# A value mix moved behind the first inverse set-up, and the last chunk's steps in another order

## What is computed

```python
prev = jnp.pad(zb, ((0, 0), (1, 0), (0, 0)))[:, :T]
zb = zb + (prev - zb) * mu
r, k, v, xw, xa, xg = jnp.split(zb, cuts, axis=-1)
...
y = wkv7_scan(heads(r), heads(decay), heads(k), heads(v), -kk, kk * heads(a))
...
def step(S, inp):
    r_t, w_t, k_t, v_t, a_t, b_t = inp
    sa = jnp.einsum('bhvk,bhk->bhv', S, a_t)
    S = S * w_t[:, :, None, :] + sa[..., None] * b_t[:, :, None, :] + v_t[..., None] * k_t[:, :, None, :]
    y = jnp.einsum('bhvk,bhk->bhv', S, r_t)
    return S, y
```

## Time and profile before

| | |
|---|---|
| median of three runs | 2555.91 us (2554.29 to 2558.12) |
| the profiled execution | 2555.16 us |
| its span | 2553.4 us |
| PE busy | 2489.6 us, 98% of the span |
| DVE busy | 1428.8 us, 56% |
| ACT busy | 1093.3 us, 43% |
| POOL busy | 147.6 us, 6% |
| last slab's matmuls end | about 327 us |
| recurrence alone on the engines | about 327 to 446 us |

### The profile page before, as it was taken

How to read it: one execution, slowest core, us unless ns; L and a number is a source line. 1 busy time by engine, 2 the same in 40 slices (tenths; PEclk the granted TensorE clock), 3 DMA queues, 4 the chain that set the end, 5 groups by cost and what they waited for, 6 DMA issues and landing times.

```text
span 2553.4 us, 31712 instructions
## 1 busy us (share of the span) xinstructions
PE 2489.6 (98%) x13463; PEld 2056.5 (81%) x13463; DVE 1428.8 (56%) x1555; ACT 1093.3 (43%) x1216; POOL 147.6 (6%) x171
## 2 busy tenths in 40 slices
PE   8999999999999999999998999999999999999998
PEld 6888778778888888888777977777888888888876
DVE  5556775665445545455556667656545444545564
ACT  5445432454434334334445445554434434334442
POOL 4001224000000000000000000000000000000100
PEclk9999999999999999999999999999999999999999
DMA  8556511546565555555553654356555565555543
GB/s 262 191 180 207 172 31 69 198 170 230 182 197 181 197 188 185 190 196 182 181 181 116 207 164 151 116 165 225 190 189 192 182 197 184 194 189 190 183 169 127
DMA packets 224850, 453.22 MB, mean 177 GB/s; under 512 B 7865, under 2 KB 16375, under 8 KB 223435
## 3 DMA queue, kind: packets, MB, share of 16 engines
q1 hardware_dynamic: 219165, 430.63, 50.7%
q0 software_dynamic: 3648, 17.54, 2.2%
q10 hardware_dynamic: 1902, 3.07, 0.4%
HBM read 445.52 MB, written 2.10 MB: 175 GB/s over the span
## 4 chain that ended last, share of the span: by engine, by line
PE 92%; DVE 4%; ACT 2%; DMA 1%; issue 1%; DVEq 0%; SPq 0%; ACTq 0%
PE psum L295 28%; PE psum L297 28%; PE psum L296 28%; PE psum L780 1%; PE psum L895 1%; DMA raw<-in_w_mlp_up 1%; PE psum L1699 1%; PE psum L1708 1%; DVE wlo L284 1%; DVE uTl L437 0%; PE psum L1035 0%; PE psum L1036 0%; PE psum L1037 0%; PE psum L415 0%; ACT uTh L435 0%
## 5 line engine op out<-in xcount | busy, mean ns | idle before, releaser
L284 DVE TENSOR_TENSOR wlo<-raw,whi 128x2048 fp32r<-128x2048 f32 (+1 forms) x408 | 937.7, 2305 | 730.2 <-ACT whi L279 729.6
L279 ACT ACTIVATE whi<-raw 128x2048 fp32r<-128x2048 f32 (+1 forms) x408 | 773.9, 1902 | 760.6 <-DMA raw<-in_w_mlp_down 328.6
L295 PE MATMUL psum<-whi,uTh 128*128 128x512 f32 (+2 forms) x2176 | 857.0, 394 | 20.0 <-DVE uTl L437 12.5
L297 PE MATMUL psum<-whi,uTl 128*128 128x512 f32 (+2 forms) x2176 | 844.5, 388 | 0.0
L296 PE MATMUL psum<-wlo,uTh 128*128 128x512 f32 (+2 forms) x2176 | 844.3, 388 | 0.0
L295 PEld LDWEIGHTS psum<-whi,uTh 128*128 128x128 f32 x2176 | 411.0, 189 | 109.8 <-issue 26.9
L297 PEld LDWEIGHTS psum<-whi,uTl 128*128 128x128 f32 x2176 | 411.2, 189 | 82.0
L296 PEld LDWEIGHTS psum<-wlo,uTh 128*128 128x128 f32 x2176 | 411.5, 189 | 80.3 <-issue 2.4
L295 PE MATMUL psum<-whi,hTh 128*128 128x512 f32 x1024 | 400.1, 391 | 0.0
L297 PE MATMUL psum<-whi,hTl 128*128 128x512 f32 x1024 | 398.6, 389 | 0.0
L296 PE MATMUL psum<-wlo,hTh 128*128 128x512 f32 x1024 | 398.4, 389 | 0.0
(11 more groups left out here) (355 smaller groups left out, 1405.0 us busy)
## 6 DMA issues: line engine op xcount, KB each, us to landing
raw<-in_w_mlp_up SPq DMA_DIRECT2D x128, 1024.0 KB, 5.4
raw<-in_w_mlp_down SPq DMA_DIRECT2D x128, 1024.0 KB, 5.0
raw<-in_ab_w_in SPq DMA_DIRECT2D x48, 1024.0 KB, 5.1
raw<-in_w_ple_gate SPq DMA_DIRECT2D x32, 1024.0 KB, 5.0
raw<-in_c_w_in SPq DMA_DIRECT2D x24, 1024.0 KB, 5.3
raw<-in_ab_w_out SPq DMA_DIRECT2D x16, 1024.0 KB, 5.2
raw<-in_c_w_out SPq DMA_DIRECT2D x16, 1024.0 KB, 5.1
raw<-in_c_w_in SPq DMA_DIRECT2D x12, 736.0 KB, 4.5
```

Of the source, the lines that this page charges most:

```text
L279: act.activation(whi[:, q, :, 0:n], raw[:, q, :, 0:n], ACT.Copy).then_inc(hi_ready, 1)
L284: dve.tensor_tensor(wlo[:, q, :, 0:n], raw[:, q, :, 0:n], whi[:, q, :, 0:n].bitcast(F32), ALU.subtract).then_inc(lo_ready, 1)
L295: pe.matmul(o, xh, hi, start=(q == 0 and k == 0), stop=False)
L297: last = pe.matmul(o, xl, hi, start=False, stop=(q == 3 and k == 3))
```

## The change

Four things are changed.

1. The mix of the second half of v is taken out of its place ahead of `product_dve(0, 0, 0)`. Its subtraction and product now stand behind `level_set_dve` of tile 0, its sum behind `level_y_dve(0, 3)`. `zprev_v` moves from 24 KB to 48 KB, the home of `p_ka`, which `rwkv_early_dve` reads; so the transfers of SP and of POOL for this mix now wait for `rw_b` as well.
2. POOL no longer waits for the mix ahead of `rkr`, but for `rkba` at 8; its wait for the mix now stands ahead of `g2v`.
3. Y of tile 1 has its own PSUM banks (2 and 3), and `Us` of tile 1 its own place.
4. The steps of the last chunks are written in another order on PE, ACT and DVE.

```diff
-    zprev_v = at("zprev_v", [P, TT, W], F32, 24)
+    zprev_v = at("zprev_v", [P, TT, W], F32, 48)
...
-    Us = at("Us", [P, BW], F32, 187.5)
+    Us = [at(f"Us{tt}", [P, BW], F32, (187.5, 96)[tt]) for tt in range(TT)]
...
                 pool.wait_ge(mm_used, 4 * (base["ab_in"] + N_AB))
+                pool.wait_ge(sem("rw_b"), 1)
...
         eng.wait_ge(sem("ev_ab_in"), R0 + i + 1)
+        if i == LAST:
+            eng.wait_ge(sem("rw_b"), 1)
...
-        dve.tensor_tensor(z, z, d, ALU.add).then_inc(sem("mixed"), 1)
+        if i < LAST:
+            mix_sum_dve(dve, i)
+
+    def mix_sum_dve(dve, i):
+        _, col, n = ab_slabs[R0 + i]
+        z = zb[:, :, col:col + n]
+        dve.tensor_tensor(z, z, shift_at(i)[0][:, :, 0:n], ALU.add).then_inc(sem("mixed"), 1)
...
-    Y_BANK = 0
+    Y_BANK = (0, 2)
...
         pool.memset(Y1[0][:], 0.0).then_inc(sem("level_set"), 1)
+        pool.wait_ge(sem("rkba"), 8)
         pool.wait_ge(sem("ka_rk_in"), 32)
-        pool.wait_ge(sem("mixed"), N_AB - R0)
         pool.wait_ge(sem("ti0"), 1)
...
         pool.wait_ge(sem("bon"), 1)
+        pool.wait_ge(sem("mixed"), N_AB - R0)
...
         if tt:
-            pe.wait_ge(sem("y_out"), 1)
+            pe.wait_ge(sem("st_upd"), 2)
...
         x_first_pe(pe, 1)
         x_state_pe(pe, 2)
-        y_last_pe(pe, 0)
+        s_first_pe(pe, 1)
         u_pe(pe, 2)
-        s_first_pe(pe, 1)
         s_state_pe(pe, 2)
         s_last_pe(pe, 2)
+        y_last_pe(pe, 0)
+        x_state_pe(pe, 3)
         y_first_pe(pe, 1)
-        x_state_pe(pe, 3)
+        u_pe(pe, 3)
         y_state_pe(pe, 2)
         y_state_pe(pe, 3)
-        u_pe(pe, 3)
         y_last_pe(pe, 1)
...
         x_out_act(act, 2)
+        u_out_act(act, 2)
+        split_hi(act, base["ab_out"], 0)
         y_out_act(act, 0)
-        u_out_act(act, 2)
-        prologue(split_hi, act, "ab_out")
         x_out_act(act, 3)
+        split_hi(act, base["ab_out"], 1)
+        u_out_act(act, 3)
         y_square_act(act, 0)
-        u_out_act(act, 3)
         y_out_act(act, 1)
...
-        mix_dve(dve, link, LAST)
 
         product_dve(dve, 0, 0, 0)
-        dve.wait_ge(sem("mixed"), N_AB - R0)
         product_dve(dve, 0, 0, 1)
         dve.wait_ge(sem("level_set"), 4)
         level_set_dve(dve, link, 0)
+        mix_dve(dve, link, LAST)
...
         level_y_dve(dve, 0, 3)
+        mix_sum_dve(dve, LAST)
...
         u_out_dve(dve, 2)
+        st_dve(dve, 2)
         split_lo(dve, base["ab_out"], 0)
-        st_dve(dve, 2)
```

More of the change, by code:

```diff
@@ L1765, in s_last_pe @@
                 last = pe.matmul(bank[S_BANK[c]][half(s_), p * CH:(p + 1) * CH], av[half(h_), tt, head(p, s_)],
-                                 Us[half(h_), 512 * s_ + p * CH:512 * s_ + (p + 1) * CH], start=False, stop=(p == 7))
+                                 Us[tt][half(h_), 512 * s_ + p * CH:512 * s_ + (p + 1) * CH], start=False, stop=(p == 7))
         last.then_inc(sem("s_mm"), 1)
@@ L1774, in y_first_pe @@
         if tt:
-            pe.wait_ge(sem("y_out"), 1)
+            pe.wait_ge(sem("st_upd"), 2)
         for p, s_, h_ in lockstep():
-            last = pe.matmul(bank[Y_BANK + s_][half(h_), p * CH:(p + 1) * CH], QT[half(h_), tt, 8 * s_ + p, :],
+            last = pe.matmul(bank[Y_BANK[tt] + s_][half(h_), p * CH:(p + 1) * CH], QT[half(h_), tt, 8 * s_ + p, :],
                              vv[half(h_), tt, head(p, s_)], start=(p == 0), stop=False)
@@ L1786, in y_state_pe @@
             for s_ in range(2):
-                last = pe.matmul(bank[Y_BANK + s_][half(h_), p * CH:(p + 1) * CH], XT[tt][3][half(s_), p, half(h_)],
+                last = pe.matmul(bank[Y_BANK[tt] + s_][half(h_), p * CH:(p + 1) * CH], XT[tt][3][half(s_), p, half(h_)],
                                  ST[half(s_), (c - 1) % 2, p, :], start=False, stop=False)
@@ L1796, in y_last_pe @@
         for p, s_, h_ in lockstep():
-            last = pe.matmul(bank[Y_BANK + s_][half(h_), p * CH:(p + 1) * CH], PT[half(h_), tt, 8 * s_ + p, :],
-                             Us[half(h_), 512 * s_ + p * CH:512 * s_ + (p + 1) * CH], start=False, stop=(p == 7))
+            last = pe.matmul(bank[Y_BANK[tt] + s_][half(h_), p * CH:(p + 1) * CH], PT[half(h_), tt, 8 * s_ + p, :],
+                             Us[tt][half(h_), 512 * s_ + p * CH:512 * s_ + (p + 1) * CH], start=False, stop=(p == 7))
         last.then_inc(sem("y_mm"), 1)
@@ L1951, in u_out_act @@
             act.wait_ge(sem("u_mm"), 2 * c + 1 + s_)
-            act.activation(Us[half(c % 2), 512 * s_:512 * s_ + 512], bank[X_BANK[c // 2] + s_][half(c % 2), :],
+            act.activation(Us[c // 2][half(c % 2), 512 * s_:512 * s_ + 512], bank[X_BANK[c // 2] + s_][half(c % 2), :],
                            ACT.Copy).then_inc(sem(f"u_out{s_}"), 1)
@@ L1957, in y_out_act @@
         act.activation(zb[:, tt, 0:BW].rearrange("p (a s c) -> p s a c", s=2, c=CH),
-                       pair_of(Y_BANK).rearrange("p (s a c) -> p s a c", s=2, c=CH), ACT.Copy).then_inc(sem("y_out"), 1)
+                       pair_of(Y_BANK[tt]).rearrange("p (s a c) -> p s a c", s=2, c=CH), ACT.Copy).then_inc(sem("y_out"), 1)
     a4 = lambda x: x[:].rearrange("p t (f c) -> p t f c", f=2)
@@ L2083, in u_out_dve @@
         dve.wait_ge(sem("u_mm"), 2 * c + 2)
-        dve.tensor_copy(Us[half(c % 2), 512:1024], bank[X_BANK[c // 2] + 1][half(c % 2), :]).then_inc(sem("u_out1"), 1)
+        dve.tensor_copy(Us[c // 2][half(c % 2), 512:1024], bank[X_BANK[c // 2] + 1][half(c % 2), :]).then_inc(sem("u_out1"), 1)
     def st_dve(dve, c):
```

## The result

The changed kernel takes 2561.64 us, median of 10 runs (2559.22 to 2566.43), against 2554.47 us for the kernel before in 10 runs on the same chip. That is inside the forecast range, 2552.5 to 2563.5, but the likeliest time, 2558.8, was 2.8 too low, the loss is more than twice the 2.9 us that I forecast, and the change passes the 0.2% up to which I had called it "same" with a chance of 0.84. So the sign and the mechanisms have to be told apart from the size.

What follows compares the result with a forecast made beforehand. PE is always busy from 470 us, so recurrence time counts only through PE's last wait, for DVE's split_lo at 462.79. +2.24 (front) and +0.65 (last chunks) give +2.9 us: 2555.91 becomes 2558.8, range 2552.5 to 2563.5.

Steps and rivals of the forecast that it cites:

- rival (c): At rkr: POOL gets the port before the subtraction, level_d 6.8 us later; +7.5 us, 2563.4; chance 0.1.
- The mix and POOL's `rkr`: Behind tile 0's Ti: the product waits for POOL's whole 4.53 us instruction; level_d +0.9 us instead of -2.24.
- Rival (a): At rkr: nothing holds anything, the mix is hidden; between -3.4 and -0.2 us, 2552.5 to 2555.7; chance 0.2.
- The edge: Behind Ti: DVE's subtraction is issued only 0.26 us ahead of POOL's rkr, so DVE goes first.
- The copies: At tile 0's scalings: POOL's two TTi copies slip between DVE's products, which lose 2 x 0.97 = 1.94 us.
- The first `level_d`: Head of the levels: with holding at both the copies and rkr, it begins at 355.2, +2.24 us.
- The clock behind it: First level: low clock costs about 1 us per 64 matmuls, assumed unchanged, 1.5 us either way in the range.
- rival (d): Elsewhere: stops or clock dips come to more than 5 us either way; chance 0.04 faster, 0.02 slower.
- The last chunks: PE's stop falls at u(2); PE's last step gains about 1.1 us, DVE's path loses 0.65; +0.65 taken.
- The sum: Whole kernel: +2.24 at the front plus +0.65 in the last chunks, +2.9 us, median 2558.8.
- the cases above 5 us: Whole kernel slower beyond the 0.2% limit of 5.1 us: 0.1 for POOL first, 0.02 for stops or clock dips.
- The sum at `level_y_dve(0, 3)`: The mix's sum in its new place: costs at most its own 1.2 us, taken as nothing.

Runs made afterwards that it cites:

- mix_only: Kernel before with only the mix moved and POOL's waits changed, last chunks as before; 2558.75 us against 2554.79, ratio 1.0013.
- copies_first: Changed kernel with only POOL's two copies into TTi moved ahead of its wait for rw_b; 2558.41 us in its one execution.
- after_again: The changed kernel once more, with no further edit; 2562.97 us against 2553.55 for the kernel before, ratio 1.0030.
- end_only: Kernel before with only the new Y banks, second Us and new order of the last chunks, mix in its old place; 2557.15 us, ratio 1.0011.
- the halves: Each half of the change alone against the kernel before: mix moved, ratio 1.0013; new banks, Us and last chunks' order, ratio 1.0011.
- the repaired front: Changed kernel's front with POOL's copies ahead of its rw_b wait and rkr behind the first level_y_dve of tile 1; 1.0002 new order, 1.0001 old.
- fixed_front: Changed kernel with POOL's copies ahead of its rw_b wait and rkr behind the first level_y_dve of tile 1; 2554.49 us against 2554.79, ratio 1.0002.

## Why the prediction was right in its mechanisms and short in its size

That the measured time lies inside the range is in part luck. The upper end of the range was set by rival (c), which did not come, and the forecast path ended at 2.9 us of loss. What filled the room between is the clock, which the sum held at nothing.

**The mix and POOL's `rkr`: right.** Forecast: subtraction at full speed, POOL in between, the product to wait for all of its instruction. Measured: 1.18, 5.31 and 5.43 us in this order. Rival (a), that nothing holds, would have needed a product of 2 us or less; rival (c), POOL first, a subtraction over 4. Neither came. The edge that I had put at 0.26 us was 0.25 or 0.26 in each of the profiles in which `rkr` stands there. "SBUF — State Buffer" in the Trainium skill, section "Who interferes with whom", says that the shared port is held exclusively; the cut `rkr` (2.17 against 5.43, same elements) agrees with it over a factor of four in length.

**The copies: right, one instruction short.** I had two scalings delayed by 1.94 together. Three were, by 0.47 + 0.83 + 0.83 = 2.1, since the copies began 0.61 us behind the first scaling and not 0.1. The first `level_y` came 0.7 earlier, where I had 0.9.

**The first `level_d`: right in size.** +2.24 forecast, +2.5 measured; of the 0.3 between them 0.2 is the scalings. `rkr`'s 5.31 where I had 4.53 adds almost nothing: it counts from 0.26 behind the subtraction's start and holds the wait for it, and it ended 0.2 later than I had it, on the same scale.

**The clock behind it: the first step that failed.** I wrote that the low clock stands behind the decay matmuls in any case, "so I leave it, with 1.5 us either way". That looked at the price of a low level, but not at what sets it: I had PE idle for some 3 us ahead of `level_d` in my own walk and did not ask what the clock does behind such a hole. It took 2.9 us more by the fourth `level_y`. Against the kernel before, which has 3.4 us of low clock there too, the term was -1.5 in the execution of `mix_only`, +2.9 in the first profile of the full change and in `copies_first`, and +4.1 in `after_again`; and my "1.5 us either way" is in neither end of the range, which are (a) and (c) without it. Over the region the clock was at half for 10.2 us before and 23.9 after. Nearest to this came rival (d), clock dips of more than 5 us, which I had looked for elsewhere and given 0.02.

**The last chunks: the second step that failed.** The place of the stop was forecast rightly, at `u(2)` (it came two matmuls ahead of it, at the end of `s_first`). Its size and the clock behind it were not. I carried over the 1.17 us and took +0.65 for the whole part; `end_only` measured +2.8 (0.5 to 4.9 by the interval). Three rows account for it. The stop is 1.91 (2.19 in `end_only`). The matmuls behind it ran at half clock: 3.35 us for 58 of `y_last(0)` that I had at 2. And ACT's copy of Y, which I had ending at 437.1, hangs on them: the copy ends at 447.06 in the changed kernel, 15.3 behind the 431.76 of the earlier trace rows. Of this 6.5 is what the front and the start had cost, and 8.8 is left where I had 5.3. PE's last step of the recurrence ends 454.39 against 445.66, that is +8.7, less the same 6.5 = +2.2; I had -1.1. In `after_again`, with a stop of 1.27 and the clock high, the same differences from the fourth `level_y` on are +5.7 for ACT's copy, -0.9 for PE's last step and +1.1 for the end of the wait for `wlo`: there the walk holds. So what failed is not the order of the steps but the missing clock term behind a stop that is often longer than 1.17. In the changed kernel PE then waits 3.38 us for `uTl` and 1.05 for `wlo`:

```profile
473.46 0.47 PE L1035 MATMUL psum<-whi,uTh 128*128 128x512 f32 x1 [1.05 <-DVE wlo L284]
```

I had this wait end near 465.7. About 1.6 of the difference comes back at once, since no low clock follows the wait; before, 3.4 us of it began at 463.6, and it now stands earlier, behind the wait for `uTl`.

**The sum.** Forecast +2.24 + 0.65 = +2.9; measured by the halves +3.3 and +2.8, and together +7.9. The 1.8 between 6.1 and 7.9 is within the intervals, and I can't say that it is an interplay. It fits with the clock, whose low stretches behind the front and in the last chunks differ from one execution to the next: in the ten runs of the changed kernel the time follows the mean granted clock, 2566.43 us at 0.990 and 2559.22 at 0.993.

**The chances.** The mechanism that came was the one with the highest chance, but I spread its size by too little, and the cases above 5 us had 0.12 in all. The sum at `level_y_dve(0, 3)` cost nothing, as forecast.

**What stays open.** What PE stops for in the last chunks. Why the 2.2 us that the repaired front gains don't show in the time. In `fixed_front` its profile gives them back in the last chunks. But with the old order the profile's region is 1.7 us shorter than before (141.5), and the median is 1.0001 (0.9991 to 1.0010) all the same; a gain of 2.2 us lies at the very end of this interval, so it isn't excluded. And whether a filling of the right length would gain anything.

## What to carry to other kernels

Before a DVE instruction with two SBUF inputs is moved into a hole, look at what POOL begins at that moment and how long its longest single instruction is: that length, not the share of the work, is the price. Cutting POOL's instruction in four left 0.9 us of 4.2 here, and delaying it by one wait left nothing. Where a walk leaves PE idle for some microseconds inside a chain of small matmuls, give the clock a term of its own; behind a hole of 3 us it was -1.5 to +4.1 us here, and one profile doesn't tell which. Take a second profile of the same kernel before its loss is divided among causes. An unexplained stop of PE that recurs at the same place is part of the cost of a reordering: ask which step it will stand ahead of.

## What the runs showed of the hardware that I had not expected

- A DVE product of 1.23 us took 5.42 or 5.43 us in all executions in which POOL's 2048-column product began behind the subtraction, and 2.17 beside 512-column ones.
- Behind 3.01 us of PE idling ahead of small matmuls, the clock was low at once in the changed kernel, in `copies_first` and in `after_again` (13.7 us long in the last, by its clock records), but not in `mix_only`. In the execution with PE kept busy it was high (2.08 us for the level against 3.68).
- One fp32 product with 512 columns shows as two matmuls in the trace, 12 for six products and 5.42 us.
- PE's stop without a releaser in the last chunks varied from 1.17 to 2.19 us between executions with the same loads. When half of the transfers beside it were moved away it was still there (1.91 us in the new order, 0.88 in the old), and a stop of 1.12 us came in both orders where the transfers had gone.
- The same order of the last chunks took 94.0 us in one execution and 97.1 in another of the same kernel, with a granted clock of 1.00 and 0.57 in one and the same stretch of it.
